# The output products of two attention blocks: waits by pair, the odd block's first slab ahead of the last pair's values, and a conditioning vector's chunks moved on VectorE

## The reference

```python
def even_layer(...):     # Fourier mixing beside attention with 8 heads
    q_l = mla_q(q_a, q_norm, w_qb, rope)
    a_l = blocked_dense_attention(q_l, concat(k_c, k_l), concat(v_c, v_l), MLA_SCALE)
    y_l = concat(fourier_mix(f_in) * silu(f_gate), a_l * silu(m_gate)) @ w_out

def odd_layer(...):      # 16 heads on 4 key heads, a sink, a band of 128 tokens
    y_l = (windowed_gqa(q, k, v, ck, cv, sink) * silu(g)) @ w_out

def first_block(...):
    for l in range(2):
        sh, sc, g = split(silu(c) @ w_mod[l] + b_mod[l])
        h = rmsnorm(x, norm_g[l]) * (1 + sc) + sh
        x = x + g * y_l(h)
```

## Time and profile before

| what | us |
|---|---|
| median of 3 runs (lowest, highest) | 1382.53 (1378.92, 1384.83) |
| the profiled execution's own time | 1377.82 |
| its span | 1376.0 |
| PE busy in the span | 1302.6 (95%) |
| PEld, DVE, ACT, POOL busy | 1075.3, 950.1, 499.4, 151.1 |
| mean granted clock of TensorE | 0.991 of full speed |

### The profile page before, as it was taken

The page is one execution under the profiler, slowest core; times in us unless marked ns, Lnnn a source line. Parts: engine busy times, 40 slices in busy tenths (PEclk is TensorE's granted clock), DMA queues, the critical chain, the costliest instruction groups (busy, mean ns, idle before and its releaser), DMA issues.

```text
span 1376.0 us, 19017 instructions
## 1 busy us (share of the span) xinstructions
PE 1302.6 (95%) x7913; PEld 1075.3 (78%) x7913; DVE 950.1 (69%) x1221; ACT 499.4 (36%) x769; POOL 151.1 (11%) x168
## 2 busy tenths in 40 slices
PE   5999999999988999999998999999999999899996
PEld 2798656447955469889887898986988998789895
DVE  4867767658677765877788666666577778754546
ACT  3322146123355043443333434324344333343432
POOL 2201100100000110013321000001001232000000
PEclk9999999999999999999999999999999999999998
DMA  9643540426510675577765677536557684455551
GB/s 356 240 150 105 198 131 1 153 71 205 199 62 1 213 265 171 180 258 248 295 231 177 232 244 247 191 125 255 181 179 255 249 309 164 153 184 184 183 185 60
DMA packets 104911, 257.77 MB, mean 187 GB/s; under 512 B 8213, under 2 KB 11766, under 8 KB 104570
## 3 DMA queue, kind: packets, MB, share of 16 engines
q1 hardware_dynamic: 80432, 171.75, 36.8%
q0 software_dynamic: 20192, 75.58, 15.1%
q10 hardware_dynamic: 4202, 9.23, 1.9%
HBM read 255.49 MB, written 1.05 MB: 186 GB/s over the span
## 4 chain that ended last, share of the span: by engine, by line
PE 76%; DVE 12%; ACT 4%; DMA 3%; issue 3%; POOL 1%; POOLq 0%; SPq 0%; DVEq 0%; ACTq 0%
PE bank L767 74%; DVE weights_low L2144 2%; PE bank L928 2%; DMA weight_ring<-in_w_in_dram 2%; DMA start_ring<-in_w_mod_dram 1%; ACT odd_prob L1758 1%; DVE negated_maxima L2387 1%; ACT weights_high L1568 1%; ACT even_A L1702 1%; DVE statistics L2098 1%; DVE even_A L2083 1%; DVE x L2097 1%; DVE xn L2091 1%; DVE x L2618 1%; POOL inverse_roots L666 1%
## 5 line engine op out<-in xcount | busy, mean ns | idle before, releaser
L2144 DVE TENSOR_TENSOR weights_low<-weight_ring,weights_high 128x2048 fp32r<-128x2048 f32 (+1 forms) x124 | 272.5, 2200 | 224.8 <-ACT weights_high L1568 224.7
L1568 ACT ACTIVATE weights_high<-weight_ring 128x2048 fp32r<-128x2048 f32 (+1 forms) x124 | 227.5, 1837 | 391.5 <-PE bank L767 328.8
L767 PE MATMUL bank<-uT_high,weights_high 128*128 128x256 f32 (+1 forms) x1200 | 341.2, 284 | 6.5 <-issue 2.7
L767 PE MATMUL bank<-uT_low,weights_high 128*128 128x256 f32 (+1 forms) x1200 | 339.5, 283 | 0.0
L767 PE MATMUL bank<-uT_high,weights_low 128*128 128x256 f32 (+1 forms) x1200 | 339.4, 283 | 0.0
L767 PEld LDWEIGHTS bank<-uT_high,weights_high 128*128 128x128 f32 (+1 forms) x1200 | 228.3, 190 | 11.8 <-ACT gate_tanh L1899 6.7
L767 PEld LDWEIGHTS bank<-uT_low,weights_high 128*128 128x128 f32 (+1 forms) x1200 | 228.4, 190 | 1.0
L767 PEld LDWEIGHTS bank<-uT_high,weights_low 128*128 128x128 f32 (+1 forms) x1200 | 228.4, 190 | 0.5
L1986 DVE SCALAR_TENSOR_TENSOR modulation_sums<-modulation_ring,silu_c_columns,modulation_sums 128x1024 f32<-128x1024 f32 x112 | 148.7, 1328 | 15.4 <-DMA modulation_ring<-in_w_ada_dram 7.8
L767 PE MATMUL bank<-weights_high,hidden_high 128*128 128x512 f32 x256 | 101.7, 397 | 1.1 <-DVE weights_low L2144 1.1
L767 PE MATMUL bank<-weights_low,hidden_high 128*128 128x512 f32 x256 | 101.2, 395 | 0.0
(11 more groups left out here) (311 smaller groups left out, 2166.0 us busy)
## 6 DMA issues: line engine op xcount, KB each, us to landing
weight_ring<-in_w_in_dram SPq DMA_DIRECT2D x52, 1024.0 KB, 6.7
modulation_ring<-in_w_ada_dram POOLq DMA_DIRECT2D x48, 1024.0 KB, 6.9
weight_ring<-in_w_up_dram SPq DMA_DIRECT2D x32, 1024.0 KB, 5.4
weight_ring<-in_w_down_dram SPq DMA_DIRECT2D x32, 1024.0 KB, 5.0
modulation_ring<-in_w_mod_dram POOLq DMA_DIRECT2D x16, 1024.0 KB, 5.4
weight_ring<-in_o_w_in_dram SPq DMA_DIRECT2D x10, 1024.0 KB, 5.3
weight_ring<-in_w_branch_dram SPq DMA_DIRECT2D x16, 512.0 KB, 3.7
weight_ring<-in_w_o_dram SPq DMA_DIRECT2D x8, 1024.0 KB, 7.0
```

What stands on the lines that cost most here:

```text
L767: return track(pe.matmul(*args, **kw))
L1568: act.activation(ring[:, s, c0:kn * cols], wring[:, slot, c0:kn * cols], ACT.Copy).then_inc(S["high_ready"], 1)
L2144: dve.tensor_tensor(lo[:, s, c0:kn * cols], wring[:, slot, c0:kn * cols], hi[:, s, c0:kn * cols].bitcast(F32), ALU.subtract).then_inc(w_fr ...
```

## The change

It has four parts. (1) On DVE, chunk 1 of vector 4 goes from ahead of the rotation of `qb` to behind it. (2) `eout0` no longer waits for all eight chunks of `even_yT` at its head: only the Fourier part is waited for there, and each head pair k just ahead of its first use. (3) `tokens_out_by_tile` waits for each tile's bank when it comes to that tile, no longer for all at its head. (4) In the odd block, `keep_busy` ahead of the values of pair 6 is gone, and those values get bank 3 in place of bank 7; the first slab of `oout0` (pairs 0 to 3, both tiles) goes ahead of the values of pair 7; the second slab waits for its pairs one by one; and the four chunks of vector 7 go from behind the loop into its last two steps on DVE.

```diff
         if p >= 2:
-            jobs += [(("OPV", p - 2), last)]
+            jobs += [(("OPV", p - 2), (3,) if p == GPAIRS else last)]
...
             def tokens_out_by_tile(names, jobs, src, between=lambda i: None):
-                outs = [start(j) for j in jobs]
-                for i, o in enumerate(outs):
+                for i, job in enumerate(jobs):
+                    o = start(job)
...
             for g in range(4):
                 copied(("f2", g))
-                copied(("PV", g))
...
-            tokens_out(both("eout0"), [("eout", 0, i) for i in range(TALL)], eyT_tokens, COLS)
+            tokens_out(both("eout0"), [("eout", 0, i) for i in range(TALL)], eyT_tokens, COLS,
+                       wait=lambda k: copied(("PV", k - 4)) if k >= 4 else None)
...
+            def first_pairs(i, o):
+
+                for k in range(4):
+                    copied(("OPV", k))
+                    ins = multiply(o[:, :], oyT_tokens(k, i), cut(slab("oout0", 0), k, 0, COLS),
+                                   start=(k == 0), stop=False)
+                if i == TC - 1:
+                    used(ins, "oout0", 0)
+
...
                     pv = start(("OPV", a))
-                    if p == GPAIRS:
-                        keep_busy(pv, 4)
+                    if p == GPAIRS + 1:
+                        oout = [start(("oout", 0, i)) for i in range(TC)]
+                        for i in range(TC):
+                            first_pairs(i, oout[i])
...
-            for g in range(8):
-                copied(("OPV", g))
...
-            tokens_out(both("oout0"), [("oout", 0, i) for i in range(TC)], oyT_tokens, COLS)
+            w = slab("oout0", 1)
+            for i, o in enumerate(oout):
+                for k in range(4, KD):
+                    if i == 0:
+                        copied(("OPV", k))
+                    ins = multiply(o[:, :], oyT_tokens(k, i), cut(w, k - 4, 0, COLS), start=False, stop=(k == KD - 1))
+                done(ins, ("oout", 0, i))
+            used(ins, "oout0", 1)
...
-            for q in range(2):
-                gemv(4, q)
+            gemv(4, 0)
...
-            for q in range(2, 4):
+            for q in range(1, 4):
                 gemv(4, q)
...
+                if p == GPAIRS:
+                    for q in range(2):
+                        gemv(7, q)
+                if p == GPAIRS + 1:
+                    gemv(7, 2)
                 if 1 <= p <= GPAIRS:
                     o = ready(("OPT", p - 1, 0, 0))
...
-            for q in range(4):
-                gemv(7, q)
+            gemv(7, 3)
```

More of the change, by code:

```diff
@@ L916, in tokens_out_by_tile @@
                             done(ins, jobs[i])
-                        if i == len(outs) - 1:
+                        if i == len(jobs) - 1:
                             used(ins, *names[h])
@@ L1197, in _, with oyT_tokens @@
             pe.wait_ge(S["masks_ready"], 1)
+            def oyT_tokens(k, i):
+                return oyT[:, k, P * i:P * i + P]
+            def first_pairs(i, o):
[5 more added lines that the diff above has]
+                    used(ins, "oout0", 0)
             for p in range(GPAIRS + 2):
@@ L1252, in _ @@
                     reduce_part(6)
-            for g in range(8):
-                copied(("OPV", g))
-            def oyT_tokens(k, i):
-                return oyT[:, k, P * i:P * i + P]
-            tokens_out(both("oout0"), [("oout", 0, i) for i in range(TC)], oyT_tokens, COLS)
+            w = slab("oout0", 1)
[6 more added lines that the diff above has]
+            used(ins, "oout0", 1)
             tokens_out_by_tile(both("oout1"), [("oout", 1, i) for i in range(TC)], oyT_tokens)
```

## The result

Measured beside the kernel before, six runs each: 1371.66 us against 1380.09 us (medians; 1369.59 to 1373.56 against 1377.42 to 1384.83), a ratio of 0.9939, interval 0.9925 to 0.9953. The profiled execution took 1369.59 us, its span is 1367.8 us, its mean granted clock 0.992.

A forecast was written before the change was run, and what follows sets the result against it. PE held 76% of the chain, so time comes off only where PE stands still or does unneeded work. The terms 1.47 + 1.40 + 1.05 + 1.30 = 5.2 us, taken from 1382.5, gave 1377.3 us, range 1372.5 to 1382.0.

The forecast's parts named there:

- the base: Time the gain was taken from: the median of the runs, 1382.53 us, not the profiled execution's 1377.82.
- Part 1: Second half of the query products: PE starts at 165.84 instead of 167.31, behind ACT's copy; 1.47 us, bounds 0.9 and 1.5.
- the median row: Landing time for vector 4's last chunk: 5.4 us after issue, at 182.94, so the key copies lose nothing.
- Parts 2 and 3: Even output products: PE's waits ahead of their first and second halves go, 1.40 and 1.05 us.
- Part 4: End of odd block: 3.9 us without the copy's wait; some 2.5 us waiting for DVE's copy leaves 1.3 us.
- The clock falls behind the new wait: Rival, odd block: a clock fall after PE's 2.5 us wait takes 1.7 us, giving 1379.0 us; chance 0.25.
- The whole promise: Rival, odd block: DVE's copy does not hold PE up, sum 7.8 us, 1374.7; chance 0.23 together with the spared falls.
- The spared falls: Rival: removed waits at 165 and 247 cost other executions a clock fall; 6.9 us, 1375.6; 0.23 with the whole promise.
- A chunk late: Rival, second odd slab: vector 7's third chunk lands late, 4.9 us lost, 1382.2, or slower at 1384; chance 0.07.

The follow-up runs named there:

- the first job: The changed kernel timed against the kernel before, six runs each: 1371.66 us, ratio 0.9939.
- third profile: Profile from the third timing of the changed kernel, nothing edited, six runs beside the kernel before: 1372.41 us, ratio 0.9954.
- first profile: Profile from the first timing of the changed kernel against the kernel before: the profiled execution took 1369.59 us, the median was 1371.66 us.
- the second: Profile from the second timing of the changed kernel, nothing edited, six runs beside the kernel before: 1372.09 us, ratio 0.9952.
- chunks behind the values: Changed kernel with chunks 0 and 1 of vector 7 moved behind DVE's values of pair 6, timed twice: 1371.97 and 1368.60 us, 0.9949 and 0.9934 of before.
- the last kernel's: Changed kernel with chunks 0 and 1 behind the values of pair 6, plus four unread products ahead of those values: 1368.47 us, 0.9924 of before.
- The two kernels with the longest waits of PE: Changed kernel with DVE's copy of the first turned result ahead of two vector 7 chunks, 1.0001 of before; with all four chunks behind the loop, 1.0015.

## Why the prediction was wrong

**The step that failed is the base.** "The median of the runs is 1382.53, and I forecast 1382.5 - 5.2 = 1377.3." That median was of three runs. Over the 93 runs with a clock, the kernel before takes 1362.65 + 14.4 + 1.8 (outside the span) = 1378.9 us on the mean, so the base was 3.6 us too high; the changed kernel's 18 runs have a mean of 1372.05. The 8.4 us of the first job are this difference of 6.8 us, with the kernel before 1.2 us above its mean there (1380.09) and the changed kernel 0.4 below. Of the 5.6 us between forecast and measurement, 3.6 are the base, 0.6 the work and waits (5.8 against 5.2), 1.0 the falls, and 0.4 the first job's six runs. The split between the work and the falls is the rough one of the table. The same text had a base that would have done: against the profiled execution, "that is 1372.6". That would have been luck in part, as 1377.82 lies 1 us below the mean. It was set aside as the fastest of four, which was taken for a sign that it was off; the range, though it named 2 to 3 us for a small sample, put its lower end there.

**The terms.** The third profile of the changed kernel and that of before have no fall of the clock between 160 and 475, so their PE rows can be set against each other. Before, beside those of the earlier trace rows:

```profile
290.92 1.04 PE L928 MATMUL bank<-constants,odd_xn 128*128 128x128 f32 x8
...
435.73 2.20 PE L928 MATMUL bank<-constants,odd_prob 128*128 128x128 f32 x16
```

After, in the third profile, and DVE ahead of the key copies in the first:

```profile
157.57 7.92 PE L767 MATMUL bank<-weight_ring,even_latentsT 128*128 128x384 f32 x24
166.27 21.71 PE L767 MATMUL bank<-weight_ring,even_latentsT 128*128 128x384 f32 x56 [0.78 <-ACT even_A L1626]
...
287.10 1.04 PE L928 MATMUL bank<-constants,odd_xn 128*128 128x128 f32 x8
...
431.03 2.20 PE L928 MATMUL bank<-constants,odd_prob 128*128 128x128 f32 x16
```

```profile
189.80 1.49 DVE L2282 COPY even_E<-bank 96x512 f32<-96x512 f32 x2 [1.86 <-PE bank L928]
```

- Part 1, 1.47 us forecast. From the first query half's start to the second's: 10.07 us before (167.31 - 157.24), 8.70 after (9.31 in the profile shown, with the clock's 0.61 in its first half). 1.37 us. ACT ended the wait; in the first profile its copy ended at 165.13 + 0.49, and PE started 0.26 us later, where the prediction took 0.15. The chunk that was moved cost nothing: the last chunk's data were there at 182.94, as worked out from the median row, and DVE was idle for 1.86 us ahead of the key copies.
- Parts 2 and 3, 1.40 and 1.05 us forecast. Both waits went whole; `eout0` and `eout1` became one group. From the start of the second query half to the first turn behind these products PE took 123.61 us before (167.31 to 290.92) and 120.83 after (166.27 to 287.10): 2.78 us, against 2.45.
- Part 4, 1.30 us forecast, made of 3.9 us less a new wait of some 2.5 us for the copy behind two chunks. The wait was 2.56 and 2.57 us in the first and third profile, at the instruction named, and 0.94 in the second, with the fall ahead of it. From the turns of pair 6 (435.73 before, 431.03 in the third profile) to the end of the odd products PE took 41.42 us before and 40.31 after, with no fall in either: 1.11 us.

Together 5.3 us (1.37 + 2.78 + 1.11), the forecast 5.2. So the waits were sized right. In this pair PE also took 0.9 us less from 290.92 to 435.73, which no part touches; over three profiles of each kernel that stretch has 143.9 to 145.5 us after and 144.4 to 145.1 before, so it is chance.

About 0.5 us of the 5.8 lie elsewhere. One candidate: in all three profiles of the kernel before, a slab of `w_in` issued at about 649 landed some 12 to 13 us later and ended the chain there:

```profile
649.00 12.20 DMA weight_ring<-in_w_in_dram
```

It is on the chain in none of the changed kernel's three. From SP's issue there to its next one of the same kind, 17.00, 17.56 and 18.14 us passed before, and 15.74, 15.86 and 15.94 after, so 1.1 to 2.4 us were won there. That is more than the 0.5; where the rest goes is not shown. The two profiles of one kernel, chunks behind the values, differ in it too (15.95 and 16.86), and POOL's issue beside it follows SP's by 4.39 us in the profile of before as in that of after (648.07 and 652.46, 641.66 and 646.05). Why it lands earlier, and whether the change has a part in it, is open.

**The rivals.** *The clock falls behind the new wait*: in the changed kernel's three profiles it fell once as the wait ended (441.1), once ahead of it (438.8), and once not at all; with the wait filled, or gone, a fall stood in that stretch too, in each profile but the last kernel's. So the fall does not need that wait, and where falls lie changes from one execution to the next. *The whole promise*: could not have come by the route named. If the copy had not held PE up, bank 3 would have; that wait was overlooked. With both gone, PE took 433.40 to 471.06, 37.66 us, for what took 41.42: 3.76 us, against the 3.9 worked out. *The spared falls*: no; in all three profiles of the kernel before the clock stayed at 1.00 from 160 to 430 us, so the removed waits at 165, 247 and 276 us cost no fall there. *A chunk late*: no; it had 12 us and took 5.57.

## What to carry to other kernels

Take the base of a forecast from every run known (the mean of the four was 1381.0, still some 2 us too high), and when a median of three and the profiled execution differ by as much as the effect, forecast the difference and widen for the base. When work moves ahead of another engine's queue, list every bank and buffer that engine frees behind it, not only the first that bites: here a second wait of the same size stood behind the first, and two instructions further on in DVE's order cost neither. And when PE's work is reordered, follow what the other engine owes the next stage: with the slab moved and the chunks left, a lead of 5.7 us became a wait of 9.18 us.

## What the runs showed of the hardware

Kernels that are nearly the same lost 12.5 to 16 us to falls of the clock on the mean, by the estimate above, and which stretches fell differed between two profiles of one kernel: here the clock decides ratios within 0.2% as much as the edits do. A fall ahead of a wait for another engine cost nothing (6.47 us with it and without it); with the wait gone, a fall at the same place cost 1.49 us (5.30 against 3.81). The two kernels with the longest waits of PE in or behind the odd block (5.11 and 9.18 us) show 17.4 and 20.3 us of falls, some 3.1 of the latter inside the wait in its profile. With unread products in a wait of 2.04 us the clock stayed at 1.00 there in the one profile taken, where it fell in eight of nine without them; such products in the wait behind it did nothing for a fall that had begun ahead of them.
